# Two-transformer-block kernel: the first modulation round in two halves of channels, with the first weight block's groups begun between them, and x and ctx on two other DMA queues

## What is computed

```python
sc, scc = silu(c), silu(c_ctx)
sh1x, s1x, ... = split(sc  @ ada_w[0] + ada_b[0], 6)     # six pieces of 1024 columns
sh1c, s1c, ... = split(scc @ ada_w[0] + ada_b[0], 6)
ux = x   * (1 + s1x) + sh1x
uc = ctx * (1 + s1c) + sh1c
u  = [ux; uc] @ ab_w_in          # 512 tokens x 3616 columns, the mixer's input product
```

## Time and profile before

| | |
|---|---|
| median of 3 runs | 2488.91 us (2488.91 to 2494.91) |
| profiled execution, its own time | 2483.01 us |
| its span | 2481.2 us |
| TensorE (PE) busy | 2251.5 us, 91% of the span |
| stage 1 and the wait for column block 0 | from 0 to 41.6 us |
| stage 2 on TensorE | from 41.6 to 247.6 us |

### The profile page before, as it was taken

One profiled execution on the slowest core, in us unless ns is written; L12 is line 12 of the kernel. 1 busy time (PEld: TensorE's weight loads), 2 busy tenths in 40 slices (PEclk: granted clock), 3 DMA queues, 4 the chain that ended last, 5 costly groups with the idle time before them and its releaser, 6 DMA issues. The chain is left out here.

```text
span 2481.2 us, 35139 instructions
## 1 busy us (share of the span) xinstructions
PE 2251.5 (91%) x14031; PEld 1215.5 (49%) x14032; DVE 935.9 (38%) x1642; ACT 368.4 (15%) x631; POOL 139.2 (6%) x205
## 2 busy tenths in 40 slices
PE   6999868898888889986799999997999999989999
PEld 2443744443333324444433333333566777757776
DVE  3875667330000009868643111113433233582001
ACT  1000413111111101015111111110160000110000
POOL 1001010000000002010000000001201010000000
PEclk8999988999999999998799999999999999999999
DMA  9768521899999995890399999998316786425442
GB/s 359 287 242 333 170 71 68 347 423 423 423 423 423 423 418 199 287 341 1 150 408 422 422 422 422 421 422 319 121 60 234 258 306 238 165 85 167 152 153 71
DMA packets 174201, 687.10 MB, mean 277 GB/s; under 512 B 13813, under 2 KB 72182, under 8 KB 111649
## 3 DMA queue, kind: packets, MB, share of 16 engines
q1 hardware_dynamic: 159280, 622.24, 64.3%
q0 software_dynamic: 11824, 52.04, 5.7%
q10 hardware_dynamic: 3008, 11.62, 1.4%
HBM read 670.99 MB, written 13.81 MB: 276 GB/s over the span
## 5 line engine op out<-in xcount | busy, mean ns | idle before, releaser
L1668 PE MATMUL bank<-ring,arena 128*32 128x512 f32 (+1 forms) x3072 | 340.3, 596 | 27.8 <-DMA ring<-moe_w_up 15.3
L527 PE MATMUL bank<-ring,actT 128*128 128x512 f32 x768 | 333.8, 596 | 7.8 <-issue 3.3
L3004 PE MATMUL bank<-actT,ring 128*128 128x256 f32 x1344 | 293.4, 379 | 0.0
L3004 PEld LDWEIGHTS bank<-actT,ring 128*128 128x128 f32 x1344 | 255.2, 190 | 42.3 <-issue 8.6
L1701 PE MATMUL bank<-arena 128*32 128x512 f32 (+1 forms) x2048 | 226.7, 594 | 21.3 <-ACT arena L1812 21.3
L1880 DVE TENSOR_TENSOR arena<-arena,bank 128x512 f32<-128x512 f32 x32 | 22.0, 687 | 582.3 <-ACT arena L1807 582.3
L527 PEld LDWEIGHTS bank<-ring,actT 128*128 128x128 f32 x768 | 145.7, 191 | 194.2 <-issue 190.3
L1668 PEld LDWEIGHTS bank<-ring,arena 128*32 128x32 f32 x3072 | 99.6, 110 | 262.8 <-issue 261.8
L616 DVE SCALAR_TENSOR_TENSOR arena<-ring,cols,arena 128x2048 f32<-128x2048 f32 x80 | 185.8, 2349 | 55.6 <-DMA ring<-ada_w 54.3
L2361 PEld LDWEIGHTS bank<-arena 128*128 128x128 bf16 x2304 | 133.3, 100 | 44.5 <-issue 36.0
L3016 PE MATMUL bank<-ring,arena 128*128 128x512 f32 x352 | 154.6, 593 | 0.0
(11 more groups left out here) (513 smaller groups left out, 2200.9 us busy)
## 6 DMA issues: line engine op xcount, KB each, us to landing
ring<-moe_w_gate SPq DMA_DIRECT2D x128, 1024.0 KB, 21.1
arena<-moe_w_down SPq DMA_DIRECT2D x128, 1024.0 KB, 22.8
ring<-ada_w SPq DMA_DIRECT2D x69, 1024.0 KB, 7.5
ring<-ffn_w SPq DMA_DIRECT2D x66, 1024.0 KB, 5.4
ring<-moe_w_up SPq DMA_DIRECT2D x64, 1024.0 KB, 23.4
actT<-moe_w_up SPq DMA_DIRECT2D x64, 1024.0 KB, 24.6
arena<-ada_w POOLq DMA_DIRECT2D x27, 1024.0 KB, 9.4
ring<-ab_w_in SPq DMA_DIRECT2D x14, 1024.0 KB, 7.8
```

The lines of the kernel that those rows point to most:

```text
L527: mm = nc.tensor.matmul(self.bank[g % 6][:, :], lhsT(m, k), halves[k // 4][:, k % 4, :], start=(k == 0), stop=(k == KT - 1))
L1668: mm = nc.tensor.matmul(bank[j // 2][Q * q:Q * q + Q, :], A(XS + P * kt + Q * q, Q), weights(j, own, q, k * DE, DE), start=(kt == 0), stop ...
L3004: mm = nc.tensor.matmul(bank[2 - 2 * (j % 2) + which][:, f * SEQ:(f + 1) * SEQ], w[:, k, f * P:(f + 1) * P], self.actT[:, k * T:k * T + SE ...
```

## The change

The first round is loaded and made as four quarter products, each of two loads: (half of the channels) x (shift or scale). Loads 0 to 3 are the first half of the channels, 4 and 5 column block 0 of `ab_w_in`, 6 to 9 the second half; all ten now have 2 KB pieces. From load 10 on the list is as before. TensorE: two quads, then all eight groups of transposes of x and ctx (now in two banks by turns, waiting for ScalarE), two quads, the bias-free sum turned by a product with a picking matrix, then the first four groups' matmuls for channel blocks 0 to 3 (`first_half`), with the second half's quads between them, then the second sum. Stage 2's first four groups make only blocks 4 to 7. VectorE adds the bias after the turning, from `ada_b` laid out with 16 columns per partition, and modulates half of `actT` in stage 1, half in stage 2. x goes on ScalarE's queue, behind the bias and the rest of `k_misc`; ctx goes on GpSimd's queue, after a wait for the vectors and the identity.

```diff
--- before.py
+++ after.py
@@ -408,12 +408,12 @@
             given += n
         return share
 
-    def plan_hosting(self, w, starts, order, rounds, on_pe=(), lead=0, first=1, late=0, aside=0):
+    def plan_hosting(self, w, starts, order, rounds, on_pe=(), lead=0, first=1, late=0, aside=0, begun=False):
 
         share = self.hosted(rounds, len(order), on_pe, late, aside)
         units = [(l, r, k) for l, r in rounds for k in range(KT)][aside:]
         asked = self.asked(order, lead, first)
-        for ci in range(first):
+        for ci in range(1 if begun else 0, first):
             self.plan_linear(w, starts[ci], starts[ci] + 512)
         for g in range(len(order)):
             if g in asked:
@@ -433,7 +433,7 @@
 
         return (self.I["ada_w"], self.I["ada_w_2"])[l // 2][l % 2][k * P:(k + 1) * P, 2048 * r:2048 * (r + 1)]
 
-    def st_linear_hosting(self, lhsT, groups, dest, rounds, sums, homes, pick, on_pe=(), lead=0, first=1, late=0, lag=1, aside=(), unmix=None, tables=None, beside=None, turned=None, front=None):
+    def st_linear_hosting(self, lhsT, groups, dest, rounds, sums, homes, pick, on_pe=(), lead=0, first=1, late=0, lag=1, aside=(), unmix=None, tables=None, beside=None, turned=None, begun=None, front=None):
 
 
 
@@ -504,7 +504,10 @@
                     front["mix"](pe)
                 asked = self.asked(groups, lead, first)
                 begins = {ci: self.used + 2 * ci for ci in range(first)}
-                self.used += 2 * first
+                if begun is None:
+                    self.used += 2 * first
+                else:
+                    begins = {0: begun}
                 for g, (ci, m) in enumerate(groups):
                     if g in asked:
                         begins[asked[g]] = self.used
@@ -521,11 +524,12 @@
                     halves = [self.slot(a), self.slot(a + 1)]
                     if g >= 6:
                         pe.wait_ge(*out_of(g - 6))
-                    for k in range(KT):
+                    rest = begun is not None and ci == 0
+                    for k in range(4 if rest else 0, KT):
                         if turned is not None and g in (0, 2):
-                            pe.wait_ge(turned.sem, turned.at(4 * g + k + 1))
+                            pe.wait_ge(turned.sem, turned.at(2 * g + k - 3))
                         mm = nc.tensor.matmul(self.bank[g % 6][:, :], lhsT(m, k), halves[k // 4][:, k % 4, :],
-                                              start=(k == 0), stop=(k == KT - 1))
+                                              start=(k == 0), stop=(k == KT - 1), skip_group_check=rest)
                     mm.then_inc(self.pe_done.up(), 1)
                     if g == last_of[ci]:
                         self.frees(a, self.pe_done)
@@ -589,7 +593,7 @@
             @block.vector
             def _(dve):
                 if turned is not None:
-                    self.modulate_turned(dve, turned)
+                    self.modulate_turned(dve, turned, 1)
                 if front is not None:
                     front["vector"](dve, self.linker(dve, self.dve_chain))
                 if unmix is not None:
@@ -781,30 +785,51 @@
 
         nc, I, A, bank, sm = self.nc, self.I, self.A, self.bank, self.sem
         vecs = [I["c"], I["c_ctx"], I["c_2"], I["c_ctx_2"]]
-        RAW, BIAS, SUM = 21504, 4096, 4608
+        RAW, PICK, BIAS, SUM = 21504, 4096, 4160, 4608
         SHIFTS, SCALES = 416, 432
         vec_in, bias_in, x_in, x_turned, raw_ready, sum_done, sum_ready, sum_turned = (sm[n] for n in (
             "vec_in", "bias_in", "x_in", "z_turned", "zT_ready", "ada_done", "ada_added", "turned"))
-        turn_to = lambda n: bank[n % 6]
+        turn_to = lambda n: bank[4 + n % 2]
+        rows = lambda s, n: (self.xres[64 * s:64 * s + 64, :].rearrange("p (t d) -> p t d", t=4), I[n][0].rearrange("(t p) d -> p t d", p=64))
         with self.stage() as block:
             @block.tensor
             def _(pe):
-                def unit(k):
+                def quad(h, third, q):
                     self.arrived(pe, self.used)
                     sl = self.slot(self.used)
                     for j in range(4):
-                        mm = nc.tensor.matmul(bank[6][32 * j:32 * j + 32, :], self.scx[:, 32 * k:32 * k + 32],
-                                              sl[:, 0, 512 * j:512 * j + 512], start=(k == 0), stop=(k == KT - 1))
-                    c = sum_done if k == KT - 1 else self.weights_used
+                        mm = nc.tensor.matmul(bank[6 + third][32 * j:32 * j + 32, :], self.scx[:, 32 * (4 * q + j):32 * (4 * q + j) + 32],
+                                              sl[:, j, :], start=(q == 0), stop=(q == 1))
+                    c = sum_done if q else self.weights_used
                     mm.then_inc(c.up(), 1)
                     self.frees(self.used, c)
                     self.used += 1
 
+                def add_and_turn(h):
+                    if h == 0:
+                        pe.wait_ge(raw_ready.sem, raw_ready.at(8))
+                    for third in range(2):
+                        pe.wait_ge(sum_ready.sem, sum_ready.at(2 * h + third + 1))
+                        for b in range(4):
+                            mm = nc.tensor.matmul(bank[4 + h][:, P * third + 32 * b:P * third + 32 * b + 32], A(SUM + 512 * third + b * P, P),
+                                                  A(PICK, 32), start=True, stop=True)
+                    mm.then_inc(sum_turned.up(), 1)
+
+                def first_half(m):
+                    w = self.slot(4)
+                    if m == 0:
+                        self.arrived(pe, 4)
+                    for k in range(4):
+                        if m % 2 == 0:
+                            pe.wait_ge(raw_ready.sem, raw_ready.at(8 + 2 * m + k + 1))
+                        nc.tensor.matmul(bank[m][:, :], self.actT[:, k * T + m * P:k * T + m * P + P], w[:, k, :], start=(k == 0), stop=False,
+                                         skip_group_check=True)
+
                 def turn_x(t):
                     for g in range(2):
                         n = 2 * t + g
-                        if n >= 6:
-                            pe.wait_ge(raw_ready.sem, raw_ready.at(n - 5))
+                        if n >= 2:
+                            pe.wait_ge(raw_ready.sem, raw_ready.at(n - 1))
                         for q in range(4):
                             k = 4 * g + q
                             mm = nc.tensor.transpose(turn_to(n)[:, q * P:(q + 1) * P], self.x_tile(t)[:, k * P:(k + 1) * P], self.ident)
@@ -813,32 +838,34 @@
                 pe.wait_ge(vec_in.sem, vec_in.at(80))
                 nc.tensor.transpose(bank[7][:, 0:32], self.arena[0:32, RAW:RAW + P], self.ident[0:32, 0:32]).then_inc(self.pe_done.up(), 1)
                 pe.wait_ge(self.dve_done.sem, self.dve_done.at(1))
-                for k in range(5):
-                    unit(k)
-                pe.wait_ge(x_in.sem, x_in.at(32))
-                turn_x(0)
-                turn_x(1)
-                unit(5)
-                turn_x(2)
-                unit(6)
-                turn_x(3)
-                unit(7)
-                pe.wait_ge(sum_ready.sem, sum_ready.at(1))
-                for b in range(4):
-                    mm = nc.tensor.transpose(bank[7][:, b * P:(b + 1) * P], A(SUM + b * P, P), self.ident)
-                mm.then_inc(sum_turned.up(), 1)
+                quad(0, 0, 0)
+                quad(0, 0, 1)
+                pe.wait_ge(x_in.sem, x_in.at(16))
+                pe.wait_ge(self.params_in.sem, self.params_in.at(16))
+                for t in range(4):
+                    turn_x(t)
+                quad(0, 1, 0)
+                quad(0, 1, 1)
+                add_and_turn(0)
+                self.used += 2
+                first_half(0)
+                first_half(1)
+                quad(1, 0, 0)
+                quad(1, 0, 1)
+                first_half(2)
+                quad(1, 1, 0)
+                quad(1, 1, 1)
+                first_half(3)
+                add_and_turn(1)
 
             @block.sync
             def _(sp):
-                half = lambda s, n: sp.dma_start(self.xres[64 * s:64 * s + 64, :].rearrange("p (t d) -> p t d", t=4),
-                                                 I[n][0].rearrange("(t p) d -> p t d", p=64)).then_inc(x_in.up(16), 16)
-                self.feed(sp, 3)
-                half(0, "x")
-                half(1, "ctx")
                 self.feed(sp)
 
             @block.gpsimd
             def _(pool):
+                pool.wait_ge(vec_in.sem, vec_in.at(80))
+                self.load_params(pool, [rows(1, "ctx")])
                 nc.gpsimd.memset(self.pw[:, :], -0.5)
 
             @block.scalar
@@ -847,10 +874,10 @@
                     act.dma_start(self.arena[8 * v:8 * v + 8, RAW:RAW + P],
                                   bass.AP(tensor=src.tensor, offset=src.offset, ap=[[P, KT], [1, P]])).then_inc(vec_in.up(16), 16)
```

(48 more changed lines are left out.)

## The result

The kernel after takes 2529.43 us (median of 4 runs, 2524.24 to 2531.59) against 2489.20 for the kernel before (4 runs): a ratio of 1.0148, 95% interval 1.0129 to 1.0167, or 40.2 us slower. The forecast was 14.6 us slower, 2503.5, with a range to 2512. The direction was right, the size was not, and the time lies outside the range.

What follows compares the result with a forecast made beforehand. Stage 1 was taken as bound by what lands, stage 2 by PE. x at 31.1 plus 10.6 gave 41.7; group 4 at 85.4 plus 176.8 gave 262.2, 14.6 later; 2488.9 + 14.6 = 2503.5 us, range 2487 to 2512.

Steps and rivals of the forecast that it cites:

- x lands: Stage 1, ScalarE's queue: x arrives at 31.1 us, behind 2048 4-byte bias pieces costing 13.2 us in turns.
- x to first matmul: End of stage 1: 32 transposes, two quads, turn, link and first modulation take 10.6 us.
- second halves begin: After the first halves and the second half's four quads, PE starts the second halves at 63.1 us.
- wait at group 4: Stage 2: PE stands 8.6 us for column block 1, whose slots VectorE gives back late.
- group 4 to the end of stage 2: Rest of stage 2: takes 176.8 us as before, with the gap of 3.3 us in it.
- I found no later resource with a fixed date: After stage 2: a shift of its end at 247.59 us moves the kernel's end by as much.
- The 1.7 us for the clock at the first halves: From first matmul to second halves: 1.7 us for the lower clock after a wait, as before.
- The two turnings by picking: Turning of the sums: eight small picking products in place of four transposes, twice, priced at 0.66 us each.
- 1 (the bias passes quickly): Stage 1: many 4-byte pieces pass in one turn, bias costs 2.2 us; +2.5 us, 2491.4; chance 0.30.
- 2 (faster): Bias quick, x and ctx early at 16 us, no wait for column block 1: -9 us, 2480; chance 0.07.
- 3 (dearer pieces): Stage 1: small bias pieces cost 0.172 us each, 8.8 us more, 2512; chance 0.08.
- The first halves hide nothing: First halves, at 41.7 us: loads 6 and 7 have landed already, no weight is being waited for.

Runs made afterwards that it cites:

- Experiments 1: Kernel before with 15 small unused matmuls (60 instructions) on TensorE where it waits for load 3: 2508.02 us against 2487.97.
- 5: Kernel after with 49 unread products on TensorE while it waits for x, 252 instructions more than before: 2515.27 us.
- experiment 11: Kernel after with bias as contiguous rows, column blocks listed two groups early and 49 tiny matmuls ahead of everything: 2491.96 us, ratio 1.0002.
- the lead alone: Kernel before with each next column block of the weights listed one group earlier, nothing else: 2485.28 us, ratio 0.9981.
- 10: Kernel before with only ctx moved, to ScalarE's queue right behind the identity: 2487.49 us, ratio 0.9996.
- run 2: Kernel after with the bias as 16 contiguous rows of 512 bytes, turned together with the vectors: 2523.93 us.
- 9: Kernel before with ctx behind the identity on ScalarE's queue and column blocks listed one group earlier: 2482.19 us, ratio 0.9971.
- 6: Kernel after with bias as contiguous rows, column blocks listed two groups early and 49 unread products while TensorE waits: 2507.06 us.

## Why the prediction was wrong

Step by step, in the profiled executions:

| term of the forecast | forecast, us | measured, us |
|---|---|---|
| x lands | 31.1 | 33.5 |
| x to first matmul | 10.6 | 10.9 |
| first matmul | 41.7 | 44.46 |
| second halves begin | 63.1 | 65.65 |
| group 3 ends | 76.8 | 79.6 |
| wait at group 4 | 8.6 | 9.46 |
| group 4 to the end of stage 2 | 176.8 | 181.3 |
| stage 2 ends later by | 14.6 | 22.8 |
| everything after stage 2 | 0 | 16.7 at the skip |

22.8 + 16.7 = 39.5, against 40.2 between the medians.

**The step that failed** is "I found no later resource with a fixed date, so I take it that a shift of 247.59 moves the end by as much". I looked for resources with dates, and the new cost has none: it is the position of TensorE's instructions, which the change moves by 56. I counted every added instruction by its duration and never as a place. Experiments 1 (padding brings it) and 5 (padding takes it away) show this, and the packets on the instruction queue go with it. That a fetch takes 6 us because the DMA engines are full there (416 GB/s from 895 to 930 us before) was not tried; the packet itself took 1.0 us of the 6.2.

**The mis-sized term** in the first part is "From group 4 to the end I take what it took before": 176.8 against 181.3, 4.5 us short. I gave the lower clock a price after the start of stage 2 and none after the wait that I forecast myself. The windows of the kernel after:

```profile
89.00:92.00 3.00, 2.92 (x4) 1.40 (x5) 0.48 (x1) 0.00 (x0) 0.00 (x0) 0.50 1.00 418
92.00:100.00 8.00, 8.00 (x16) 3.41 (x16) 7.96 (x4) 0.60 (x1) 0.00 (x0) 0.82 1.00 405
```

0.50 granted, the level of 1.2 GHz, right behind 9.5 us of idleness: group 4 took 10.0 us, not 6.87. Another 1.5 came the same way behind the pause at group 20.

**x, 2.4 us late.** The mechanism, one whole turn for each small piece, was right (0.091 us measured, 0.103 taken). With ctx in the round three queues took 0.40 us for one packet each (101 packets of each from 15 to 17.5 us, 16 x 2.5 / 101; I had 0.36), and still the bias and ctx together passed 1.1 us sooner than forecast: from 8.0, the end of the identity's packets, to 24.2, the first packet of the rest of the table, 16.2 us for 17.3. The 2.4 us come from three other terms. The identity ended 1.4 us later than I had it (8.0 for 5.4 + 1.2). The rest of the table and x took 8.3 us for 6.9, since x's turns took 0.40 too (119 packets from 27 to 30 us; I had 0.345). And from x's last packet (32.5) to TensorE it was 1.0 us for 0.3.

**Inside, two errors that cancel.** The 1.7 us for the clock at the first halves did not come (7.11 us for 16 records, against 6.87 for a group). The two turnings by picking took 1.97 and 1.87 us where I had 0.66 each: I priced eight f32 matmuls (16 records) by four transposes (4 records). The second modulation is waited for 1.4.

**The wait at group 4** was right in kind: SyncE could issue at 75.03 and 79.68 where I had the second at 77.4, and the load landed 9.4 us later where I had 8.

**What I did not see but cost nothing:** ScalarE is held until 13.6 us by the issues behind the bias, so the first quads come at 16.3. They had time, since x was later still.

**The rivals.** 1 (the bias passes quickly) is out: one turn each. 2 (faster) never came near: x was late and the wait at group 4 there. 3 (dearer pieces) is out by 0.091 us. "The first halves hide nothing" held: at 44.46 us no load was waited for, and experiment 11, no faster than the lead alone, bears it out.

## To carry to other kernels

Before a change adds instructions to an engine that is the bound, look for branches over long bodies in what follows, and compare the branch's duration before and after as the first thing: padding with idle instructions, here 49 tiny products in a wait, tells in one run whether a loss belongs to the edit or to its place. A transfer with 4-byte pieces costs one turn of its neighbour's packet for each, whatever its bytes, and whatever is queued behind it on its engine waits too. Give each forecast wait on TensorE a second price for the clock behind it, and ask first whether a prefetch asked for one group earlier removes it: here that gave some 4 us and the whole restructuring, repaired, none.

## What the runs showed of the hardware

- A branch of TensorE over a long body took 0.2, 6 or 12 us by the place of the code. 56 to 60 instructions more made the second of two branches 12 us, 252 more gave 0.2 back; 15 to 17 us for the program. In the first layer a branch of 6 us had one packet of 16,384 bytes on the instruction queue, one of 12 us three, one of 0.2 us none.
- A pause of 3.3 us in full work was followed by a granted share of 1.00, 0.86 or 0.70 over 190 to 200 us, in three kernels alike in that stretch (before, 10 and 1).
- Behind a DMA of 2048 pieces, whose own issue took 0.62 us, the next two issues on ScalarE's queue took 7.6 and 2.2 us, against 0.5 and 0.7 without it (run 2).
- Two transfers to 64 partitions each, one on SyncE's queue and one on ScalarE's, moved 306 and 295 GB/s from 10 to 20 us (9 and 10) where both on SyncE's queue moved 243 (before).
- A product of 128 x 32 took 0.38 us while TensorE did nothing else (49 in 18.4 us in 5; 21.1 us, 0.43 each, in 6), one of 32 x 2 took 0.11 (49 in 5.38).
